# Two stacked blocks on one core: the small products of the recurrences grouped by form, SiLU on ScalarE, a later gate, and fewer drains

## The reference

```
# first block: gated linear attention (4 heads), a short convolution, window attention, merge, gated FFN
attn = where(causal, (q e^(b-bref)) (k e^(bref-b))^T, 0);  o = attn v + (q e^b) state
y_gla = (norm(o) * silu(gr)) @ w_gla_o
# second block: 16 meta tokens in front; two mixers side by side, then a gated FFN
qa = silu(q); f = lb + (1-lb) sigmoid(f_pre); o = HGRN2(qa, 1-f, log f, i);  out_a = norm(o) * silu(g)
xbc = silu(conv4(xbc)); dt = softplus(dt_pre + bias)
y = SSD(x dt, exp(cumsum(dt a)), B, C) + D x;  out_b = groupnorm(y * silu(z))
h = h + concat(out_a, out_b) @ w_out
```

## Time and profile before

| | |
|---|---|
| Runs before | 1750.24, 1750.38, 1752.63 us; median 1750.38 |
| Profiled execution | 1751.12 us, of which the span is 1749.3 us |
| Granted TensorE clock | 0.998 of full speed |
| TensorE / VectorE / ScalarE busy | 99% / 66% / 42% |

### The profile page before, as it was taken

One profiled execution on the slowest core, in us unless ns is written; L12 is line 12 of the kernel. 1 busy time (PEld: TensorE's weight loads), 2 busy tenths in 40 slices (PEclk: granted clock), 3 DMA queues, 4 the chain that ended last, 5 costly groups with the idle time before them and its releaser, 6 DMA issues.

```text
span 1749.3 us, 27505 instructions
## 1 busy us (share of the span) xinstructions
PE 1734.1 (99%) x11080; PEld 1530.1 (87%) x11080; DVE 1159.8 (66%) x1796; ACT 729.4 (42%) x1119; POOL 14.5 (1%) x18
## 2 busy tenths in 40 slices
PE   9999999999999999999999999999999999999998
PEld 7888887788888888888899999999998999999887
DVE  5766656566568777734476766778788877777332
ACT  6444433332353333333545454554554433333221
POOL 0000000000000000000000000000000000000000
PEclk9999999999999999999999999999999999999999
DMA  5222332223333333333222222222222233323331
GB/s 193 85 78 79 90 95 81 85 75 96 96 97 97 96 97 96 108 98 97 77 81 73 61 73 70 65 73 73 73 61 73 85 97 97 97 88 94 103 98 64
DMA packets 45773, 153.82 MB, mean 88 GB/s; under 512 B 6064, under 2 KB 8496, under 8 KB 45648
## 3 DMA queue, kind: packets, MB, share of 16 engines
q1 hardware_dynamic: 44816, 151.29, 28.7%
q10 hardware_dynamic: 832, 0.79, 0.1%
HBM read 149.96 MB, written 2.10 MB: 87 GB/s over the span
## 4 chain that ended last, share of the span: by engine, by line
PE 92%; DVE 4%; ACT 1%; issue 1%; DVEq 1%; ACTq 0%; DMA 0%; POOL 0%; SPq 0%; POOLq 0%
PE ps L713 91%; PE ps L717 2%; DVE arena L1539 2%; ACT arena L1115 1%; DVEq L2116 1%; DVE w_lo L1536 0%; DVE arena L1546 0%; DVE h_res L1536 0%; DVE arena L1553 0%; ACTq L1519 0%; DMA h_res<-xT 0%; DVE arena L1542 0%; DVE u_lo L1774 0%; POOL ffn L693 0%; ACT w_hi L1115 0%
## 5 line engine op out<-in xcount | busy, mean ns | idle before, releaser
L713 PE MATMUL ps<-u_hi,w_hi 128*128 128x258 f32 (+3 forms) x2376 | 638.9, 322 | 1.4 <-DVE h_res L1536 1.4
L713 PE MATMUL ps<-u_lo,w_hi 128*128 128x258 f32 (+3 forms) x2376 | 633.5, 320 | 0.8 <-DVE u_lo L1774 0.8
L713 PE MATMUL ps<-u_hi,w_lo 128*128 128x512 f32 (+3 forms) x2352 | 625.7, 319 | 0.0
L1536 DVE TENSOR_TENSOR w_lo<-w_raw,w_hi 128x1024 fp32r<-128x1024 f32 (+1 forms) x279 | 340.2, 1219 | 147.9 <-ACT w_hi L1115 135.8
L713 PEld LDWEIGHTS ps<-u_hi,w_hi 128*128 128x128 f32 (+1 forms) x2376 | 394.3, 188 | 41.0 <-issue 5.1
L713 PEld LDWEIGHTS ps<-u_lo,w_hi 128*128 128x128 f32 (+1 forms) x2376 | 391.6, 187 | 34.2 <-DVE u_lo L1774 1.6
L1115 ACT ACTIVATE w_hi<-w_raw 128x1024 fp32r<-128x1024 f32 (+1 forms) x281 | 294.2, 1047 | 301.5 <-PE ps L713 294.7
L713 PEld LDWEIGHTS ps<-u_hi,w_lo 128*128 128x128 f32 x2352 | 389.4, 188 | 31.2 <-issue 0.2
L1546 DVE SCALAR_TENSOR_TENSOR ffn<-full,par,ffn 128x512 f32<-128x512 f32 (+2 forms) x176 | 132.2, 751 | 80.9 <-ACT ffn L1115 77.7
L1115 ACT ACTIVATE ffn<-full,par 128x512 f32<-128x512 f32 x88 | 67.7, 770 | 264.4 <-DVE full L1539 264.4
L1115 ACT ACTIVATE arena<-arena 128x528 f32<-128x528 f32 (+10 forms) x189 | 96.2, 531 | 167.9 <-DVE arena L1539 88.4
(11 more groups left out here) (159 smaller groups left out, 1517.1 us busy)
## 6 DMA issues: line engine op xcount, KB each, us to landing
w_raw<-weights SPq DMA_DIRECT2D x278, 512.0 KB, 3.5
h_res<-xT SPq DMA_DIRECT2D x8, 256.0 KB, 5.1
outT<-h_res SPq DMA_DIRECT2D x4, 256.0 KB, 2.2
cst<-consts SPq DMA_DIRECT2D x1, 730.0 KB, 8.2
w_raw<-weights SPq DMA_DIRECT2D x2, 256.0 KB, 4.0
outT<-ffn ACTq DMA_DIRECT2D x2, 256.0 KB, 2.5
seg<-consts SPq DMA_DIRECT2D x1, 256.0 KB, 8.1
outT<-h_res SPq DMA_DIRECT2D x2, 128.0 KB, 2.5
```

The lines of the kernel that those rows point to most:

```text
L713: return nc.tensor.matmul(out, lhsT, rhs, start=start, stop=stop)
L1536: return V.tensor_tensor(out, a, b, op)
```

## The change

- Small products by form: in `head_a` all products of one width follow each other, then all transposes. Products that contracted over 16 or 32 rows now contract over all 128, over tiles whose other rows are zero: `pre`, the meta products of `head_b`, `head_c`, `ssm_b`, `ssm_c`, and the `pick` products of `ssm_a`, which now all read the whole of `ac_st`. The zeros are written once: by GpSimd at the start and at the start of the second block, and by VectorE in `ssm_zero`.
- SiLU by ScalarE: `ACT.Silu` in place of tanh, for `gr`, `hq`, `hg`, the convolutions and `mz`. VectorE's `twice_silu` for them goes, and so do "silu" steps; the taps are no longer halved. Silu lies in another table set than Exp and Ln, so `silu_table()` and `exp_ln()` load sets, placed ahead of waits.
- The gate and the square of step 4 stand one group later, and in `head_v` the wait for the gate stands just before it is used.
- ScalarE and VectorE begin no drain before the kinds that `follows_on` names.

```diff
-    ("mx", 5): "b 4; v2 0; v2 1; v2 2; v2 3; taps mx 5", ("mz", 4): "silu mx 5; c 4", ("om", (0, 0)): "v2 4",
+    ("mx", 5): "b 4; v2 0; v2 1; v2 2; v2 3; taps mx 5", ("mz", 4): "silu mx 5; c 4", ("om", (0, 0)): "gate 4; sq 4; v2 4",
...
+def follows_on(kind, i):
+    if kind == "group":
+        return GROUPS[i][0] in ("mx", "mz", "oh")
+    return kind in ("ssm_a", "ssm_am", "ssm_b", "ssm_c", "ssm_gate", "ssm_v2", "ssm_sq", "low", "taps")
...
-                mm(ps[:, 7, :], wal[0:2 * GLA_RANK, n * P:(n + 1) * P], ga_sb[0:2 * GLA_RANK, :]).then_inc(pa_ok, 1)
+                mm(ps[:, 7, :], wal[:, n * P:(n + 1) * P], ga_sb).then_inc(pa_ok, 1)
...
-                for b in range(NBLK):
-                    at = b * BLK
-                    if gla:
-                        c = GLA_C
+                starts = [b * BLK for b in range(NBLK)]
+                if gla:
+                    c = GLA_C
+                    for at in starts:
                         mm(ps[:, 4, at:at + c], kf1[:, at:at + BLK], qf1[:, at:at + c])
+                    for b, at in enumerate(starts):
                         mm(ps[0:c, 4, at + c:at + BLK], g_kL[:, b, :], g_qB[:, b, :])
                         mm(ps[c:BLK, 4, at + c:at + BLK], kf1[:, at + c:at + BLK], qf1[:, at + c:at + BLK])
+                    for b, at in enumerate(starts):
                         turn(ps[:, 5, at:at + BLK], g_kZ[:, b, :])
+                    for at in starts:
                         last = turn(ps[:, 6, at:at + BLK], vf1[:, at:at + BLK])
-                    else:
+                else:
+                    for b, at in enumerate(starts):
                         for c in range(SUB):
                             q0, n_k = META + at + HG_C * c, HG_C * (c + 1)
                             mm(ps[HG_C * c:n_k, 4, at:at + n_k], qd2[:, q0:q0 + HG_C], KC[:, b, c * BLK:c * BLK + n_k])
+                    mm(ps[0:META, 7, 0:16], kcm[:, 0, :], qd2[:, 0:META])
+                    for b, at in enumerate(starts):
                         turn(ps[:, 5, at:at + BLK], KC[:, b, SUB * BLK:(SUB + 1) * BLK])
...
-                    mm(ps[:, 7, 272:400], h_ktm[0:META, :], h_vtm[0:META, :])
+                    mm(ps[:, 7, 272:400], h_ktm, h_vtm)
...
-                    last = mm(ps[:, 7, 400:416], h_vtm[0:META, :], h_am[0:META, :])
+                    last = mm(ps[:, 7, 400:416], h_vtm, h_am)
...
+                every = [pick[:, 2 * t + i:2 * t + i + 1].broadcast_to((P, P)) for i in range(2)]
                 for i in range(2):
-                    rows, h = slice(32 * i, 32 * i + 2 * M2_H), 2 * t + i
-                    mm(ps[:, 4 + i, :], pick[rows, h:h + 1].broadcast_to((2 * M2_H, P)), ac_st[rows, META:T2])
+                    mm(ps[:, 4 + i, :], every[i], ac_st[:, META:T2])
...
-                mm(ps[:, 7, 160:288], m_btm[0:META, g, :], m_xtm[0:META, 1, :])
+                mm(ps[:, 7, 160:288], m_btm[:, g, :], m_xtm[:, 1, :])
...
-                    last = mm(ps[rows, 7, 288:304], m_xtm[0:META, 0, rows], m_atm[0:META, i, :])
+                    last = mm(ps[rows, 7, 288:304], m_xtm[:, 0, rows], m_atm[:, i, :])
...
+            def silu_table():
+                if table[0] != ACT.Silu:
+                    nc.scalar.preload_act_table_set("silu_and_others")
+                    table[0] = ACT.Silu
...
+                silu_table()
                 act.wait_ge(ssm_sem["conv"], CONV_NO[which])
-                f(cv[1], cv[0], ACT.Tanh).then_inc(silu_ok, 1)
+                f(x, cv[0], ACT.Silu).then_inc(ssm_sem["x"], 1)
+                if which in (("mx", 0), ("mb", 1), ("mx", 2), ("mx", 3)):
+                    exp_ln()
...
-            def conv2(which):
-                dve.wait_ge(silu_ok, FT + CONV_NO[which])
-                twice_silu(conv_tile(*which), cv[1], cv[0]).then_inc(S["x"], 1)
...
-                gate = m_z[t % 2][:, USED:]
-                link(twice_silu(gate, full[:, t % 2, USED:], gate))
                 dve.wait_ge(S["y"], t + 1)
-                half_mul(m_y[:, t, USED:], m_y[:, t, USED:], gate).then_inc(S["gated"], 1)
+                mul(m_y[:, t, USED:], m_y[:, t, USED:], full[:, t % 2, USED:]).then_inc(S["gated"], 1)
```

More of the change, by code:

```diff
@@ L699, in second_zeros @@
                 nc.gpsimd.memset(h_attn, 0.0)
+                nc.gpsimd.memset(h_ktm, 0.0)
+                nc.gpsimd.memset(h_vtm, 0.0)
+                nc.gpsimd.memset(ac_st[:, :].bitcast(F32), 0.0)
                 nc.gpsimd.memset(h_am, 0.0).then_inc(cleared, 1)
+            for rows in (slice(2 * GLA_RANK, 4 * GLA_RANK), slice(4 * GLA_RANK, P)):
+                nc.gpsimd.memset(wal[rows, :], 0.0)
+                last = nc.gpsimd.memset(ga_sb[rows, :], 0.0)
+            last.then_inc(padded, 1)
             for kind, i in STEPS:
@@ L1112, in f @@
             def f(out, in_, func, **k):
-                if func in (ACT.Tanh, ACT.Sigmoid, ACT.Silu):
+                if func == ACT.Silu or func == ACT.Tanh and table[0] != ACT.Silu:
                     table[0] = func
@@ L1149, in group @@
                 if kind in ("gr", "hg"):
-                    if kind == "gr" and i:
-                        act.wait_ge(tile_lo, TILE_NO[("y", GLA_H + i - 1)])
-                    if kind == "hg" and i:
-                        act.wait_ge(gate2_ok, i)
                     gate = g_gate[:, i % 2, :] if kind == "gr" else h_gate[:, i % 2, USED:]
+                    silu_table()
                     evacuated(act, g)
-                    f(c_a if kind == "gr" else h_thg[:, USED:], gate, ACT.Tanh, scale=0.5).then_inc(act_part, 1)
+                    f(gate, gate, ACT.Silu).then_inc(act_part, 1)
                 elif kind == "hf":
@@ L1205, in group @@
                     evacuated(act, g)
-                    f(full[:, i % 2, USED:], m_z[i % 2][:, USED:], ACT.Tanh, scale=0.5).then_inc(act_part, 1)
+                    f(full[:, i % 2, USED:], m_z[i % 2][:, USED:], ACT.Silu).then_inc(act_part, 1)
+                    if 3 <= i < M2_T - 1:
+                        exp_ln()
             def conv1(which):
@@ L1517, in _ @@
                 if kind in stages:
-                    nc.scalar.drain()
+                    if not follows_on(kind, i):
+                        nc.scalar.drain()
                     stages[kind](i)
@@ L2111, in _ @@
                       "ssm_bc": ssm_bc, "ssm_a": ssm_a, "ssm_b": ssm_b, "ssm_c": lambda t: None if t == 6 else ssm_c(t), "ssm_gate": ssm_gate,
-                      "ssm_v2": ssm_v2, "ssm_zero": ssm_zero, "taps": conv1, "silu": conv2}
+                      "ssm_v2": ssm_v2, "ssm_zero": ssm_zero, "taps": conv1}
             for kind, i in STEPS:
                 if kind in stages:
-                    V.drain()
+                    if not follows_on(kind, i):
+                        V.drain()
                     stages[kind](i)
@@ L2127, in constants @@
     rows = np.arange(P)[:, None]
[L2128 removed]
+    c[:, 384:400] = (rows % M2_H == np.arange(M2_H)[None, :]) & (rows < 2 * M2_H)
     c[:, 400:401] = -1.0 * (rows % 32 >= M2_H)
```

46 lines of the change are left out of this document (20 added, 26 removed).

## The result

The changed kernel took 1727.46 us (median of 4 executions, 1727.06 to 1727.61), the kernel before 1750.41 (median of 4); the ratio is 0.9866, 95% interval 0.9849 to 0.9883. The profiled execution took 1727.61 us with a span of 1725.6.

What follows compares the result with a forecast made beforehand. TensorE, busy 99% of the span, was taken as the bound. Its own 17.7 us plus 1.5 us less waiting made 19.2 off the profiled 1751.12, 1731.9; with the median 0.74 lower, 1731 us, range 1725 to 1738 (chance 0.64).

Steps and rivals of the forecast that it cites:

- HGRN2 `head_a`: TensorE's small products in HGRN2 heads, 8 times: fewer form changes save 0.84 us each, 6.7 us (3.6 to 8.3).
- First block's `head_a`: First block's heads on TensorE, 4 times: three form changes saved, 0.42 us each, 1.7 us (1.0 to 2.5).
- Sixteen rows made 128: `head_b`, `ssm_b` and `head_c` on TensorE: full-width instructions save 0.37, 0.37 and 0.30 us each, 8.4 us (6.5 to 9.3).
- `ssm_c`: State-space burst on TensorE: its tail keeps the 64-wide form, so nothing saved (0 to 0.8 us in all).
- Waits: TensorE's waiting: 1.5 us less (from 4 less to 5 more), with VectorE's relief, short covered drains and the later gate.
- `ssm_b(1)`: TensorE's 0.95 us wait there stays about as before: 1.4 us from VectorE pays for a 1.28 us table load.
- The later gate: State-space step 4: its square no longer delays the first half's root; counted within 1.5 us less waiting.
- The table loads: ScalarE: 16 new loads at 1.28 us each, 20.5 us, nothing added behind them, standing ahead of waits.
- the exp loads did not surface eight times: Rival: eight exp loads stand on the path between `ssm_a` and `ssm_b`, 10.2 us come back, 1741; chance 0.10.
- the narrow runs did speed up: Rival: narrow runs do not speed up, both `head_a` terms (8.4 us) go, 1739.5; chance 0.10.
- ScalarE did not become what the state-space part waits for at every step: Rival: all 16 loads lie on ScalarE's path to TensorE, 20.5 us against 19.2 saved, about 1754; chance 0.04.
- the third rival: TensorE's waits vanish altogether through VectorE's larger relief, some 3 to 4 us more, 1727.5; chance 0.12.

Runs made afterwards that it cites:

- e9: Changed kernel without the three narrower products of each block in HGRN2's `head_a`, for timing only; 1727.12 us in one execution.
- e2: Kernel before with only the 16- and 32-row products taken over 128 rows; 1745.35 us, ratio 0.9963.
- e5: Kernel before with both TensorE edits (`head_a` grouped by form, 128-row products), SiLU, gate and drains as before; 1737.20 us, ratio 0.992.
- e12: Kernel before with both TensorE edits and the change's fewer drains, SiLU still in two steps, gate at its old place; 1730.91 us.
- e4: Changed kernel with the gate and square of step 4 back at their old place; 1724.77 us, ratio 0.9849.
- e7: Changed kernel with a drain ahead of every piece of ScalarE and VectorE again; 1732.51 us.
- e11: Changed kernel with step 4's gate and square at their old place and the first half's root behind the SiLU of convolution 5 and gate 4; 1723.62 us.
- e10: Changed kernel with the narrow products of HGRN2's `head_a` written strip by strip (sub-block outside, block inside); 1733.40 us in one execution.
- e3: Changed kernel with TensorE's small products as before; SiLU by ScalarE, later gate and fewer drains left; 1749.68 us, ratio 0.9991.
- e1: Kernel before with only `head_a`'s products grouped by form; 1741.64 us, ratio 0.9945.

## Why the prediction was right, and where its terms were off

The median, 1727.46, lies in the range and 3.5 us under the point. The sum against the profiled execution was 19.2 us and came out at 23.5. What was forecast to carry the gain, fewer changes of form and full rows on TensorE, carried it; the misses of its terms nearly all went one way. The waits came out near their number by luck.

- *HGRN2 `head_a`*, predicted 6.7, measured 8.9, above its bound of 8.3: the mechanism held, the term was mis-sized. "I take 0.27, nearer the lower end": a block's narrow products cost 0.2, its lower bound of 0.22, because the widest one sets the price (e9). With two instructions of 0.11 a block that is the row's own arithmetic. The run of sixteen products took 1.0 us for the 1.1 predicted.
- *First block's `head_a`*, predicted 1.7, measured 2.9, beyond its bound of 2.5. The step "0.22 if a pair costs one full instruction" failed. The narrow part of the run is this row:

```profile
96.55 0.69 PE L726 MATMUL ps<-arena 128*64 128x64 f32 x16
```

  The eight full-width instructions ahead of it took 96.55 - 95.62 = 0.93 us, and its sixteen, with the change behind them, 97.16 - 96.55 = 0.61. Less some 0.1 for each change, eight pairs cost 0.5, 0.06 each, half of a full one. That they move 64 columns is not enough to explain it: the eight full-width ones (the row at 95.62 above) move 64 too and cost some 0.1 each. Why the narrow ones gain by it was not tried.
- *Sixteen rows made 128*, predicted 8.4, measured 8.3. `pre` 1.5 and 1.6. `ssm_a` cost 0.4 for 0.6.
- *`ssm_c`*, taken at nothing with a bound of 0.8, saved 1.2. The tail "keeps the 64-wide form" in its columns, but 16 rows of contraction are a form of their own; e2 shows the 0.15 us a step without anything else of the change.
- *Waits*, predicted 1.5 fewer, measured 1.2 fewer. The number is near and its reasoning is not. The prediction says of the work taken from VectorE that "most of it buys nothing" and that "drains are short and under cover". With the forms alone TensorE would have waited 8.2 us more (e5); dropping the drains takes 4.8 of them away (e12), SiLU's move another 6.2 (e12 to e4), and the later gate gives 1.5 back. The cover was read from a TensorE that was 22 us slower. The reading of the waits before was short as well: the largest in the state-space part was not that of line 1539 but the 1.38 us behind `ssm_a(5)` for line 1536, the one with the slow stretch behind it.
- *`ssm_b(1)`*: predicted as before, since VectorE's 1.4 us would pay for the load's 1.28. Its wait went, through the drains (e12, e7).
- *The later gate*, counted as part of the gain ("no longer delays the root"), cost 2.7 us by the medians (e4) and 3.2 by the table: a wait of 1.6 us more at `ssm_b(5)` and a slow stretch of 1.7 behind it.
- *The table loads*: right that they take 1.28 us with nothing added, as the loads at 1248.39 and 1250.87 with the next starts at 1249.69 and 1252.16 show. The Trainium skill's 2.66 us for a switch ("ScalarE: Activation LUTs", section "What ACT_TABLE_LOAD costs") is not borne out: the row behind each load starts 1.3 us behind its start. The loads surface at two places. Beside the root they cost TensorE 0.9 us (e4 against e11, by the table). Ahead of `ssm_a(7)` a load stands right behind gate 6's SiLU and ahead of `w_hi` and the exponentials, where `ssm_b(7)` now waits 1.0 us; that it is the load there was read from the trace and not tried.

The rivals: the exp loads did not surface eight times, the narrow runs did speed up, and ScalarE did not become what the state-space part waits for at every step. The time is that of the third rival (1727.5), but TensorE's waits did not vanish; it came from TensorE's own terms.

## What to carry to other kernels

When the bound engine is made faster, price its new waits as well: here more than a third of 22.5 us would have gone into waits that the profile before did not show, and drains and covered work on other engines, worth 2.3 us of waits alone, were worth 9.5 together with it. Write small products of one form one behind the other, contract over all 128 rows with zeros where only 16 are needed, and put products for different column strips next to each other: on four strips of 32 the widest was then the price of all. A step that is moved later is also moved ahead of something: look in the order of each engine for what now stands behind it.

## What the runs showed of the hardware

- Narrow products on four column strips overlapped fully when interleaved (34 instructions in 1.01 us, the 8 widest and the 2 meta ones alone in 0.99), and only in part when written strip by strip (1.76). The Trainium skill, "TensorE: Matmul & The Clock Gate", section "Architectural detail: the array is 16× 32×32, not 1× 128×128", has an array of 32x32 sub-arrays, one of which can run a product while others still load weights, and a queue that can pull weight loads ahead of products in flight. The first agrees with e9, where the work of different strips ran side by side. How far the queue reaches, and whether that is what e10 pays for, was not measured.
- All four idle times of 2.3 to 2.7 us at `ssm_b(5)` (changed, e7, e9, e10) had a stretch at 1.2 GHz with them. It began 2.1, 2.1 and 1.5 us behind the end of the first wait in the changed kernel, e9 and e10, and 0.8 us before it in e7. One of 2.1 us there (e3) had none. Of the four waits of 1.4 us behind `ssm_a(5)` one (before) had a stretch, 0.8 us behind its end, and three (e1, e2, e5) had none. What decides it was not tried.
- The two distances in the FFN, 351.1 and 353.3 us at full granted clock, are without a cause here.
